# A two-layer diffusion block on one core: two modulation units move from layer 1's differential mixer into its recurrence, where the units stand over 22 of 24 slots instead of 18

## What is computed

```python
for layer in range(DEPTH):
    mod_l = [m[:, None, :] for m in adaln_params(c, w_mod[layer], b_mod[layer])]
    mod_c = adaln_params(c_ctx, w_mod[layer], b_mod[layer])
    p_l = split_cols(modulate(x, norm1_g[layer], mod_l[0], mod_l[1]) @ w_in[layer])
    ...
    x = x + mod_l[2] * (jnp.concatenate([a_l, b_l, n_l, w_l], axis=-1) @ w_out[layer])
    x = x + mod_l[5] * squared_relu_mlp(modulate(x, norm2_g[layer], mod_l[3], mod_l[4]),
                                        w_ff1[layer], w_ff2[layer])
```

## Time and profile before

| | |
|---|---|
| median of 3 executions | 2257.51 us (2255.23 to 2259.26) |
| the profiled execution | 2260.2 us, its span 2258.3 us |
| mean granted TensorE clock | 0.957 |
| PE / PEld busy | 2078.5 us (92%) / 1734.2 us (77%) |
| DVE / ACT / POOL busy | 1000.3 (44%) / 802.6 (36%) / 693.1 us (31%) |
| chain that ended last | PE 77%, DVE 10%, ACT 6%, issue 2%, SP queue 2%, DMA 2% |
| layer 1, DA's iterations | 1582.6 to 1666.4 us |
| layer 1, HG's levels | 1727.6 to 1786.7 us |

### The profile page before, as it was taken

The page is one execution under the profiler, slowest core; times in us unless marked ns, Lnnn a source line. Parts: engine busy times, 40 slices in busy tenths (PEclk is TensorE's granted clock), DMA queues, the critical chain, the costliest instruction groups (busy, mean ns, idle before and its releaser), DMA issues.

```text
span 2258.3 us, 32056 instructions
## 1 busy us (share of the span) xinstructions
PE 2078.5 (92%) x13292; PEld 1734.2 (77%) x13292; DVE 1000.3 (44%) x1735; ACT 802.6 (36%) x1339; POOL 693.1 (31%) x567
## 2 busy tenths in 40 slices
PE   5799898989999899999999988989999888999998
PEld 3578786768877788888888866777787677778786
DVE  2535546855775621312213353444857754121222
ACT  1533333444445521312213153232454465232231
POOL 0230212112851223323323323223024523444442
PEclk8899898999999999999999998999999999999999
DMA  8230010342421121211121123010252311322322
GB/s 290 47 76 20 20 38 19 113 131 73 153 92 57 40 73 56 68 64 57 61 71 56 57 47 75 20 38 19 86 127 93 114 57 59 104 87 87 101 85 75
DMA packets 178351, 169.71 MB, mean 75 GB/s; under 512 B 29392, under 2 KB 174752, under 8 KB 178080
## 3 DMA queue, kind: packets, MB, share of 16 engines
q1 hardware_dynamic: 177408, 164.53, 24.0%
q10 hardware_dynamic: 800, 3.15, 0.4%
HBM read 159.79 MB, written 2.10 MB: 72 GB/s over the span
## 4 chain that ended last, share of the span: by engine, by line
PE 77%; DVE 10%; ACT 6%; issue 2%; SPq 2%; DMA 2%; POOL 0%; DVEq 0%; ACTq 0%; POOLq 0%
PE gp L877 53%; PE sp L1109 3%; PE sp L1260 3%; PE gp L1146 2%; PE gp L931 2%; PE tp L1126 2%; SPq L710 1%; PE sp L1100 1%; ACT nt L1474 1%; DVE small L2201 1%; PE gp L901 1%; PE op L1146 1%; PE sp L950 1%; PE op L1126 1%; PE sp L1010 1%
## 5 line engine op out<-in xcount | busy, mean ns | idle before, releaser
L788 POOL TENSOR_TENSOR wlo<-raw,whi 128x512 fp32r<-128x512 f32 x386 | 516.4, 1370 | 1291.0 <-ACT whi L1424 1290.7
L877 PE MATMUL gp<-xhi,whi 128*128 128x512 f32 (+1 forms) x1424 | 520.0, 365 | 35.1 <-DVE xlo L1990 21.4
L877 PE MATMUL gp<-xhi,wlo 128*128 128x512 f32 (+1 forms) x1424 | 506.5, 356 | 0.0
L877 PE MATMUL gp<-xlo,whi 128*128 128x512 f32 (+1 forms) x1408 | 502.8, 357 | 0.0
L877 PEld LDWEIGHTS gp<-xhi,whi 128*128 128x128 f32 x1424 | 277.5, 195 | 83.3 <-issue 14.8
L1424 ACT ACTIVATE whi<-raw 128x2048 fp32r<-128x2048 f32 (+1 forms) x100 | 187.3, 1874 | 371.1 <-PE gp L877 356.5
L877 PEld LDWEIGHTS gp<-xhi,wlo 128*128 128x128 f32 x1424 | 276.2, 194 | 39.2
L877 PEld LDWEIGHTS gp<-xlo,whi 128*128 128x128 f32 x1408 | 273.3, 194 | 38.3 <-issue 2.0
L877 PE MATMUL gp<-hhi,whi 128*128 128x512 f32 (+1 forms) x768 | 276.5, 360 | 9.6 <-issue 5.0
L877 PE MATMUL gp<-hlo,whi 128*128 128x512 f32 (+1 forms) x768 | 274.9, 358 | 0.0
L877 PE MATMUL gp<-hhi,wlo 128*128 128x512 f32 (+1 forms) x768 | 274.7, 358 | 0.0
(11 more groups left out here) (363 smaller groups left out, 3258.1 us busy)
## 6 DMA issues: line engine op xcount, KB each, us to landing
raw<-in_w_ff SPq DMA_DIRECT2D x64, 1024.0 KB, 5.3
raw<-in_w_mod SPq DMA_DIRECT2D x48, 1024.0 KB, 5.2
raw<-in_w_in SPq DMA_DIRECT2D x20, 1024.0 KB, 5.3
raw<-in_w_in SPq DMA_DIRECT2D x24, 256.0 KB, 4.7
bias<-e SPq DMA_DIRECT2D x96, 32.0 KB
raw<-in_w_out SPq DMA_DIRECT2D x12, 256.0 KB, 3.0
xin<-in_x ACTq DMA_DIRECT2D x1, 2048.0 KB, 9.7
raw<-in_w_out SPq DMA_DIRECT2D x16, 128.0 KB, 3.3
```

The lines of the kernel that those rows point to most:

```text
L788: nc.gpsimd.tensor_tensor(wlo[:, s % 2, ks, :], raw[:, index[splits[s]] % 2, ks, :], whi[:, s % 2, ks, :].bitcast(F32), ALU.subtract)\
L877: mm = pe.matmul(out, lhs, rhs, start=(i == 0 and j == 0), stop=(i == KT - 1 and j == 2))
```

## The change

In layer 1, DA gets 5 modulation units instead of 7, HG gets 11 instead of 9, and HG's units are spread over 22 slots instead of 18. Nothing is computed differently.

```diff
--- before.py
+++ after.py
@@ -154,7 +154,7 @@
 def fill_plan():
...
-    counts = {("NA", 0): 0, ("SW", 0): 0, ("DA", 0): 12, ("HG", 0): 12, ("NA", 1): 0, ("SW", 1): 0, ("DA", 1): 7, ("HG", 1): 9}
+    counts = {("NA", 0): 0, ("SW", 0): 0, ("DA", 0): 12, ("HG", 0): 12, ("NA", 1): 0, ("SW", 1): 0, ("DA", 1): 5, ("HG", 1): 11}
@@ -176,7 +176,7 @@
...
-            span = (11 * n // 12 if l == 0 else 3 * n // 4) if m == "HG" else n
+            span = 11 * n // 12 if m == "HG" else n
```

## The result

The changed kernel takes 2263.80 us (median of 14 executions, 2259.16 to 2268.02), the kernel before 2256.73 us (14 executions, 2249.85 to 2260.42). The ratio is 1.0034, its 95% interval 1.0024 to 1.0044: slower by 7.7 us (5.4 to 9.9). The ratio is not that of the two medians, which lie 7.1 us apart; 7.7 us is its excess over 1, times 2256.73. The forecast was +5.7.

A forecast was written before the change was run, and what follows sets the result against it. PE was taken to bound the kernel as a whole, but the exponentials or DVE at some places touched. Terms -1.7 + 2.4 + 3.7 + 1.3 = +5.7 us gave 2263.2 us on the median, range 2258.0 to 2267.0.

The forecast's parts named there:

- DA, -1.7: In layer 1's DA: two rows and two turns fewer, k steps moved; -1.7 us, bounds -3.0 and -1.2.
- The levels, +2.4: In HG's levels: the new turn at level 20 waits for `mrow`, so level 21 starts later; +2.4 us, bounds +1.5 and +3.8.
- the turn at slot 22: Late in HG's levels: adds 0.4 us, which can go into the 0.82 us of idle before the last weighing.
- Behind the levels, +3.7: After the last weighing: ACT's late high part of `outA` 0 delays `project(0)` and `add(0)`; +3.7 us, bounds +3.2 and +4.9.
- the clock, +1.3: In `project(0)`: PE's 3.85 us pause lowers the clock, hitting some 7 of its last 12 matmuls; +1.3 us, bounds 0 and +2.8.
- the end of `project(0)` at W + 8.7: Behind HG's levels: `project(0)` ends 8.7 us after the last weighing (W), as POOL's parts release PE's steps.
- rival 1: Behind HG's levels: the late high part is hidden, only DA and the levels count; +0.7 us, chance 0.20.
- rival 2: Before the key transposes: later `project(0)` closes PE's pause and the clock gains; -4.9 us in all, chance 0.05.
- rival 3: From the pause before `project(0)` on: the clock stays at half speed through `project(0)` and `project(1)`; +9 us, chance 0.08.
- Rival 4: Whole change: the move does nothing, DVE's and ACT's chain sets DA's iterations, ACT's copy is early enough; +1 us, chance 0.07.

## Why the prediction was right, and where it was not

The time, its sign and its main cause came out; the sum fits better than its terms.

- **DA, -1.7.** Slot by slot it is right: 3, 6, 10, 5, 9 and 12 gave -0.70, -1.07, -1.09, +0.49, +0.10 and +0.36 against -0.7, -1.1, -1.1, +0.5, +0.3 and +0.4; with the rest -1.85 over the iterations, with the clock equal. As a whole DA gave back 0.3 to 0.7 us in the changed kernel's own profile (97.52 against 97.77 and 98.23), and nothing on the mean of the profiles: +0.7 us, a figure that five profiles between 94.79 and 100.55 leave uncertain by more than 1 us. The step that failed is that the clock's term was looked for behind the levels only: in four of these five profiles low clock within DA, some 64 us into it or at its end, took back some or all of the 1.85 us. Whether the shorter iterations bring it about is open.
- **The levels, +2.4.** Measured +3.1, inside its bounds. The wait for `mrow` was 0.91 (said 0.8), level 21 starts 2.5 us late (2.4), level 20 keeps its place behind level 18 (4.86 us, before 4.85). Mis-sized was the turn at slot 22: it costs 0.6, and the 0.82 before the last weighing takes in none of it, since that is DVE's masking of the diagonal, which starts only when PE has made it.
- **Behind the levels, +3.7, and the clock, +1.3.** `add(0)` came 4.97 us later, which is their sum to the tenth, and `project(0)` waited 3.78 us (said 3.9). But that the sum fits is luck: with the pause filled the late part alone makes 4.3, not 3.7, and the clock 0.65, not 1.3. Mis-sized was the end of `project(0)` at W + 8.7: POOL's second part was ready at W + 6.3, not at W + 5.9, and two thirds of the matmuls stood behind it. The clock's fall hit 7 matmuls, as said, but the first 7, where half of its cost lies in a wait for POOL anyway. But the keys came only 3.84 later: I had let the chain behind `add(0)` stay at 7.94 us "with POOL's low part of unit 1 beside it as before", and POOL was nearly through by then (6.81). The clock's fall is real, but filling its pause moved the keys by nothing in the changed kernel (17.05 against 16.98 us), so its own term should have been about 0 there.
- **Rivals.** The late part is not hidden (rival 1). Of rival 2 the mechanism exists and was worth 3.7 and 2.1 us in the two runs that filled the pause, but the change closes the pause before the keys only from 6.03 to 4.75 us, so it does not reach it. The longer low clock of rival 3 was seen in part only, at its longest where the high part was late in the kernel before (12 of the 18 matmuls, 11.07 us to `add(0)`). Rival 4 is excluded by the levels and the tail.

In sum +0.7 + 3.1 + 3.8 = +7.6, where -1.7 + 2.4 + 5.0 was forecast. Two errors against each other (DA +2.4, the tail -1.2) and the levels' 0.7 make the 1.9 us between them. That +7.6 meets the measured +7.7 so closely is luck as well, given what DA's mean leaves open. What is shown is the levels' +3.13 and the tail's +3.84, which make 7.0.

## What to carry to other kernels

When filler is moved, look at what stands behind it in the in-order queues of the other engines: here a filler's last row decided when a weight's buffer came free, and ACT's copy slid behind a read-out that waits for PE. A read-out that waits for an engine should have nothing behind it that this engine waits for, and a filler whose second half needs such a copy should not be placed right behind the product that is read out. Compare stretches between two events of the same kernel and clock, not totals, when the effect is a few tenths of a per cent; and try whether a pause ahead of PE-bound work is worth filling.

## What the hardware showed that I had not expected

- Beside POOL's subtractions a DVE operation loses up to about 1 us, however short it is: copies of 0.16 to 0.21 us took 1.22 to 1.26, a subtraction of 0.68 took 1.62, a scaling of 0.95 took 1.93, and a difference of 0.96 took 2.05. One of POOL's parts took 1.26 to 1.74 us there (8.36 for six). Not every operation is hit: two of the five copies kept their 0.18 and 0.21.
- Work with no use pays: 4.7 us of spare matmuls in a pause of 6.03 us raised the granted clock of the next stretch of 36 us, which had been between 0.83 and 0.86, to 1.00, and took 3.7 us off it; in a second kernel to 0.95, and 2.1 us off.
- The unchanged part ahead of DA took between 1569.3 and 1579.3 us in the fourteen profiles, whose granted clock as a whole went from 0.952 to 0.966: more than the whole effect of the change.
